# A prologue that gives every group of input rows its own landing place, splits x in chunks on two engines, and multiplies the first slot's low columns before the last parameter rows

## What is computed

```python
def rglru_mixer(x, conv_buf, h0, in_w, conv_w, conv_b, r_w, r_b, i_w, i_b, lam, out_w):
    gate, u = jnp.split(x @ in_w, 2, axis=-1)
    u, new_buf = causal_dwconv(u, conv_buf, conv_w, conv_b)
    ub = u.reshape(bsz, t, LRU_BLOCKS, LRU_BS)
    r = jax.nn.sigmoid(jnp.einsum('btnk,nkj->btnj', ub, r_w).reshape(bsz, t, LRU_W) + r_b)
    ig = jax.nn.sigmoid(jnp.einsum('btnk,nkj->btnj', ub, i_w).reshape(bsz, t, LRU_W) + i_b)
    log_a = -LRU_C * r.astype(f32) * jax.nn.softplus(-lam.astype(f32))
    ...
    y = (h.astype(x.dtype) * jax.nn.silu(gate)) @ out_w
```

## Time and profile before

| | us |
|---|---|
| median of 3 runs | 1575.88 (1572.28 to 1580.37) |
| the profiled execution | 1573.39 |
| its span, first to last instruction | 1571.7 |
| TensorE busy (matmuls) | 1434.7 (91%) |
| VectorE busy | 974.7 (62%) |
| ScalarE busy | 723.0 (46%) |
| GpSimd busy | 608.3 (39%) |
| mean granted TensorE clock | 0.940 |

### The profile page before, as it was taken

The page is one execution under the profiler, slowest core; times in us unless marked ns, Lnnn a source line. Parts: engine busy times, 40 slices in busy tenths (PEclk is TensorE's granted clock), DMA queues, the critical chain, the costliest instruction groups (busy, mean ns, idle before and its releaser), DMA issues.

```text
span 1571.7 us, 33403 instructions
## 1 busy us (share of the span) xinstructions
PE 1434.7 (91%) x12546; PEld 1306.7 (83%) x12546; DVE 974.7 (62%) x2099; ACT 723.0 (46%) x1403; POOL 608.3 (39%) x728
## 2 busy tenths in 40 slices
PE   5999889999999998888799999999999799799985
PEld 4998779888888875778789989888988599799885
DVE  4467572446555665545658778867977743646755
ACT  1577333335444444422535455454544532467721
POOL 1466343222222220146325435434445545256531
PEclk6999979999999998999799999999999799899987
DMA  3322233567667666632122414324333242222221
GB/s 119 85 74 72 65 89 109 176 196 222 214 205 226 207 193 218 196 95 76 45 73 65 114 45 125 108 69 114 108 84 95 62 116 84 81 73 79 79 58 58
DMA packets 282537, 179.72 MB, mean 114 GB/s; under 512 B 18906, under 2 KB 280826, under 8 KB 282376
## 3 DMA queue, kind: packets, MB, share of 16 engines
q1 hardware_dynamic: 282376, 177.58, 38.3%
HBM read 160.67 MB, written 16.86 MB: 113 GB/s over the span
## 4 chain that ended last, share of the span: by engine, by line
PE 57%; DVE 21%; ACT 7%; issue 6%; SPq 3%; POOL 3%; DMA 2%; DVEq 0%; ACTq 0%; POOLq 0%
PE proj L197 7%; PE proj L1755 7%; PE proj_lo L1755 7%; PE proj_lo L197 6%; PE proj L986 5%; PE proj_lo L986 4%; DVE conv L2257 3%; PE r L997 3%; PE x L1081 2%; POOL w_low L172 2%; PE s L1042 2%; DVE m L2286 1%; SPq L890 1%; PE s L1009 1%; DVE m L2302 1%
## 5 line engine op out<-in xcount | busy, mean ns | idle before, releaser
L172 POOL TENSOR_TENSOR w_low<-w_raw,w_high 128x256 fp32r<-128x256 f32 x608 | 526.2, 896 | 854.4 <-ACT w_high L163 854.4
L163 ACT ACTIVATE w_high<-w_raw 128x1024 fp32r<-128x1024 f32 x152 | 160.5, 1056 | 142.8 <-PE proj_lo L1755 51.2
L1755 PE MATMUL proj<-xh,w_high 128*128 128x288 f32 x440 | 136.3, 310 | 4.4 <-POOL w_low L172 3.0
L1755 PE MATMUL proj<-xh,w_low 128*128 128x288 f32 x440 | 131.1, 298 | 0.0
L1755 PE MATMUL proj<-xl,w_high 128*128 128x288 f32 x440 | 130.9, 298 | 0.0
L1755 PE MATMUL proj_lo<-xh,w_high 128*128 128x256 f32 x440 | 128.9, 293 | 0.0
L1755 PE MATMUL proj_lo<-xl,w_high 128*128 128x256 f32 x440 | 125.7, 286 | 0.0
L1755 PE MATMUL proj_lo<-xh,w_low 128*128 128x256 f32 x440 | 124.7, 283 | 0.0
L1755 PEld LDWEIGHTS proj_lo<-xh,w_high 128*128 128x128 f32 x440 | 84.8, 193 | 10.0 <-issue 10.0
L1755 PEld LDWEIGHTS proj<-xh,w_high 128*128 128x128 f32 x440 | 84.7, 192 | 8.5 <-POOL w_low L172 5.0
L1755 PEld LDWEIGHTS proj_lo<-xl,w_high 128*128 128x128 f32 x440 | 84.8, 193 | 0.0
(11 more groups left out here) (477 smaller groups left out, 4338.4 us busy)
## 6 DMA issues: line engine op xcount, KB each, us to landing
k_pages<-in_cache_k SPq DMA_DIRECT2D x256, 128.0 KB, 2.6
v_pages<-in_cache_v SPq DMA_DIRECT2D x256, 128.0 KB, 2.4
w_raw<-in_c_in_w SPq DMA_DIRECT2D x48, 512.0 KB, 3.9
w_raw<-in_a_in_w SPq DMA_DIRECT2D x32, 512.0 KB, 3.9
w_raw<-in_b_in_w SPq DMA_DIRECT2D x32, 512.0 KB, 4.2
w_raw<-in_a_out_w SPq DMA_DIRECT2D x16, 512.0 KB, 3.9
st<-in_state_ssd_h SPq DMA_DIRECT2D x16, 512.0 KB, 4.7
out_ssd_h_sample<-st SPq DMA_DIRECT2D x16, 512.0 KB, 6.4
```

Of the source, the lines that this page charges most:

```text
L163: act.activation(k.wh[par][:], k.raw[par][:], ACT.Copy).then_inc(k.sem["w_hi"], 1)
L172: step = pool.tensor_tensor(k.wl[par][:, tiles, :], k.raw[par][:, tiles, :], k.wh[par][:, tiles, :], ALU.subtract)
L1755: mm = pe.matmul(out, w[par][:, i, :], x[:, i, cols], start=first and opens and i == 0 and n == 0, stop=last and i == KT - 1 and n == 2, s ...
```

## The change

The twelve jobs become seven: five of x, one of both "a" groups (80 rows), one of the "c" and "m" groups (126 rows). Each lands in its own place, `k.land`, in memory that nothing else uses yet (the tile `branch`), so that SyncE waits for no transpose, and each has its own semaphore. The order of the loads is x0, x1, first weight block, x2, x3, sample rows, 14 loads of "a" rows, second weight block, 15 loads of "c" and "m" rows.

Copies of x out of PSUM are shared: VectorE takes chunks 0, 2 and 4, ScalarE 1 and 3. ScalarE rounds each chunk by itself and VectorE subtracts each by itself. TensorE transposes the five jobs of x and the "a" job, multiplies the first slot's low columns as soon as two chunks are split, transposes the "mc" job, and multiplies the high columns when all five are. ScalarE rounds the second weight block before the exponential and copies the "mc" job out of PSUM; VectorE copies the "a" job. GpSimd subtracts the second weight block ahead of its first copy of history columns (`history(0)`). The first gates' matmuls wait for ScalarE's copies out of `s`.

```diff
@@ -110,6 +110,7 @@
     k.gh, k.gl = k.g[:, 0:KT, :], k.g[:, KT:2 * KT, :]
     k.sq = [sb(f"sq{j}", [P, 2, T]) for j in range(2)]
     k.rows = [q.rearrange("p a t -> p (a t)")[:, 0:D] for q in k.sq]
+    k.land = [k.out.rearrange("p a t -> p (a t)")[:, n * D:(n + 1) * D] for n in range(7)]
     k.raw = [sb(f"w_raw{j}", [P, KT, P]) for j in range(2)]
     k.wh = [sb(f"w_high{j}", [P, KT, P], F32R) for j in range(2)]
     k.wl = [sb(f"w_low{j}", [P, KT, P], F32R) for j in range(2)]
@@ -226,36 +227,56 @@
-def row_jobs(a):
...
+X_JOB = range(CH)
+A_JOB, MC_JOB = CH, CH + 1
+A_ROWS, C_ROWS, M_ROWS = 40, 29, 10
+JOB_ROWS = [P] * QB + [NS, 2 * A_ROWS, 4 * C_ROWS + M_ROWS]
+JOB_LANDED = [f"x{c}_landed" for c in X_JOB] + ["a_landed", "mc_landed"]
+def x_rows(a, c):
+    if c == QB:
+        return [(0, NS, a["x_sample"].rearrange("b t d -> (b t) d"))]
+    return [(0, P, a["x_prompt"].rearrange("b t d -> (b t) d")[c * P:(c + 1) * P, :])]
+def a_rows(a):
+    parts = []
     for j in range(2):
+        at = A_ROWS * j
         one = [a["a_conv_b"], a["a_gate_r_b"], a["a_gate_i_b"], a["a_lambda"]]
-        jobs.append(("a", j, 40, [(0, 4, a["a_conv_w"][j])]
...
+        parts += [(at, 4, a["a_conv_w"][j])] + [(at + 4 + n, 1, v[j:j + 1, :]) for n, v in enumerate(one)]
+        parts += [(at + 8, 24, a["state_lru_conv"][j].rearrange("b k d -> (b k) d")), (at + 32, 8, a["state_lru_h"][j])]
+    return parts
+def mc_rows(a):
+    at = 4 * C_ROWS
+    parts = [(at, 4, a["ln_g"]), (at + 4, 4, a["ln_b"]), (at + 8, 2, a["c_norm_w"].rearrange("a (r d) -> (a r) d", r=2))]
     for q in range(CONV_C // D):
-        cols = slice(q * D, (q + 1) * D)
-        jobs.append(("c", q, 29, [(0, 4, a["c_conv_w"][0][:, cols]), (4, 1, a["c_conv_b"][:, cols]),
-                                  (5, 24, a["state_ssd_conv"][0].rearrange("b k d -> (b k) d")[:, cols])]))
-    return jobs
+        at, cols = C_ROWS * q, slice(q * D, (q + 1) * D)
+        parts += [(at, 4, a["c_conv_w"][0][:, cols]), (at + 4, 1, a["c_conv_b"][:, cols]),
+                  (at + 5, 24, a["state_ssd_conv"][0].rearrange("b k d -> (b k) d")[:, cols])]
+    return parts
 def prologue_sync(sp, k, a):
-    landed = [0, 0]
...
+    def rows(job, parts):
         for at, n, src in parts:
-            sp.dma_start(k.rows[j % 2][at:at + n, :], src).then_inc(k.sem[f"rows_landed{j % 2}"], 16)
+            sp.dma_start(k.land[job][at:at + n, :], src).then_inc(k.sem[JOB_LANDED[job]], 16)
+    rows(0, x_rows(a, 0))
+    rows(1, x_rows(a, 1))
+    load_slot(sp, k, 0, 0, a_slot(a, 0, 0))
+    for c in range(2, CH):
+        rows(c, x_rows(a, c))
+    rows(A_JOB, a_rows(a))
+    load_slot(sp, k, 1, 1, a_slot(a, 0, 1))
+    rows(MC_JOB, mc_rows(a))
 def a_slot(a, j, n):
@@ -276,38 +297,83 @@
     split_low(pool, k, 0, 0)
-def prologue_tensor(pe, k, a):
+def prologue_tensor(pe, k):
     sem = k.sem
+    def turn(job, parts):
+        n, bank = JOB_ROWS[job], (k.s, k.r)[job % 2]
+        pe.wait_ge(sem[JOB_LANDED[job]], 16 * parts)
+        for i in range(KT):
+            t = pe.transpose(bank[:, i // 4, (i % 4) * n:(i % 4) * n + n], k.land[job][0:n, i * P:(i + 1) * P], k.ident[0:n, 0:n])
+        t.then_inc(sem["rows_turned"], 1)
+    def first_slot(out, cols):
+        for i in range(KT):
+            for n, (w, m) in enumerate(((k.wh, k.xh), (k.wh, k.xl), (k.wl, k.xh))):
+                mm = pe.matmul(out, w[0][:, i, :], m[:, i, cols], start=i == 0 and n == 0, stop=i == KT - 1 and n == 2)
+        return mm
     pe.wait_ge(sem["consts"], 1)
-    landed = [0, 0]
...
+    turn(0, 1)
+    turn(1, 1)
+    pe.wait_ge(sem["rows_read"], 1)
+    turn(2, 1)
+    pe.wait_ge(sem["rows_copied"], 1)
+    turn(3, 1)
+    pe.wait_ge(sem["rows_read"], 2)
+    turn(4, 1)
+    pe.wait_ge(sem["rows_copied"], 2)
+    turn(A_JOB, 14)
+    pe.wait_ge(sem["w_lo"], 2)
+    pe.wait_ge(sem["x_part"], 2)
+    first_slot(k.proj_lo[:, 0:HALF], slice(0, HALF))
+    pe.wait_ge(sem["rows_read"], 3)
+    turn(MC_JOB, 15)
+    pe.wait_ge(sem["x_part"], CH)
+    first_slot(k.proj[:, 0, 0:T - HALF], slice(HALF, T)).then_inc(sem["pe_slot"], 1)
+def chunk(c):
+    return slice(c * P, min(c * P + P, T))
+def turned(k, job, at, n):
+    bank, rows = (k.s, k.r)[job % 2], JOB_ROWS[job]
+    return bank[:, :, 0:4 * rows].rearrange("p b (i n) -> p b i n", i=4)[:, :, :, at:at + n]
+def by_banks(dst):
+    return dst.rearrange("p (b i) n -> p b i n", b=2)
+def prologue_vector(dve, k, chain):
     sem = k.sem
+    def copied(c):
+        dve.wait_ge(sem["rows_turned"], c + 1)
+        dve.tensor_copy(by_banks(k.xT[:, :, chunk(c)]), turned(k, c, 0, JOB_ROWS[c])).then_inc(sem["rows_read"], 1)
+    def low(c):
+        dve.wait_ge(sem["x_split"], c + 1)
+        dve.tensor_tensor(k.xl[:, :, chunk(c)], k.xT[:, :, chunk(c)], k.xh[:, :, chunk(c)], ALU.subtract).then_inc(sem["x_part"], 1)
     dve.wait_ge(sem["consts"], 1)
-    for j, (kind, c, n, _) in enumerate(row_jobs(a)):
...
+    copied(0)
+    low(0)
+    copied(2)
+    low(1)
+    copied(4)
+    low(2)
+    low(3)
+    low(4)
+    dve.sem_inc(sem["x_ready"], 1)
+    dve.wait_ge(sem["rows_turned"], A_JOB + 1)
+    for j in range(2):
+        dve.tensor_copy(by_banks(k.par_a[j][:]), turned(k, A_JOB, A_ROWS * j, A_ROWS)).then_inc(sem["rows_read"], 1)
+    dve.wait_ge(sem["rows_read"], 5)
     for j in range(2):
         d = k.par_d[j]
         chain(dve.tensor_scalar(d[:, 0:2, :].rearrange("p c i -> p i c"), k.par_a[j][:, :, 5:7], 0.5, None, ALU.mult))
@@ -342,13 +408,31 @@
     act.activation(tmp[:, 0], tmp[:, 0], ACT.Exp, scale=-1.0).then_inc(k.sem["sp_out"], 1)
-def prologue_scalar(act, k, a):
+def prologue_scalar(act, k):
+    sem = k.sem
+    def copied(c):
+        act.wait_ge(sem["rows_turned"], c + 1)
+        act.activation(by_banks(k.xT[:, :, chunk(c)]), turned(k, c, 0, P), ACT.Copy).then_inc(sem["rows_copied"], 1)
+    def high(c, copies, count):
+        act.wait_ge(sem[copies], count)
+        act.activation(k.xh[:, :, chunk(c)], k.xT[:, :, chunk(c)], ACT.Copy).then_inc(sem["x_split"], 1)
     split_high(act, k, 0, 0, 0)
-    act.wait_ge(k.sem["rows_read"], CH)
-    act.activation(k.xh[:], k.xT[:], ACT.Copy).then_inc(k.sem["x_split"], 1)
+    copied(1)
+    high(0, "rows_read", 1)
+    high(1, "rows_copied", 1)
+    copied(3)
+    high(2, "rows_read", 2)
+    high(3, "rows_copied", 2)
+    high(4, "rows_read", 3)
+    split_high(act, k, 1, 0, 1)
     softplus_scalar(act, k, k.spa[:, :, 0:2 * KT], 1)
+    act.wait_ge(sem["rows_turned"], MC_JOB + 1)
+    for q in range(CONV_C // D):
+        act.activation(by_banks(k.par_c[:, q * KT:(q + 1) * KT, :]), turned(k, MC_JOB, C_ROWS * q, C_ROWS), ACT.Copy)
+    act.activation(by_banks(k.par_m[:]), turned(k, MC_JOB, 4 * C_ROWS, M_ROWS), ACT.Copy).then_inc(sem["rows_copied"], 1)
 def a_sync(sp, k, a, o, j, nxt):
@@ -400,17 +484,18 @@
         pe.wait_ge(sem["gw_landed"], 64 * n + 64)
         pe.wait_ge(sem["conv_done"], n + 1)
         pe.wait_ge(sem["ti_ready"], n)
+        if n == 0:
+            pe.wait_ge(sem["rows_copied"], 3)
         for g in range(2):
             pe.matmul(k.s[:, g, :], k.gw[:, g, :], k.cx[:, 0:SEQ], start=True, stop=True)
         for g in range(2):
             mm = pe.matmul(k.r[:, 0, g * NS:g * NS + NS], k.gw[:, g, :], k.cx[:, SEQ:T], start=True, stop=True)
         mm.then_inc(sem["gates_done"], 1)
-    if j == 0:
-        pe.wait_ge(sem["x_ready"], 1)
     for i in range(KT):
-        if i == 0 and j:
-            multiply_new_x(pe, k, s0, u0, 3)
+        if i == 0:
+            if j:
+                multiply_new_x(pe, k, s0, u0, 3)
         else:
             multiply_slot(pe, k, s0 + 2 * i, 0, u0 + 2 * i, u0 // 2 + i, 0, k.xh, k.xl,
                           (lambda mm: gates(i - 1)) if i else None)
@@ -520,8 +605,7 @@
         act.activation(k.gh[:, i, :], k.hg[i % 2][:], ACT.Copy).then_inc(sem["a_high"], 1)
     if j == 0:
-        act.wait_ge(sem["rows_read"], CH + 2)
-        split(1)
+        act.wait_ge(sem["rows_read"], 5)
     for i in range(KT + 1):
         if i:
             rates(i - 1)
@@ -647,9 +731,9 @@
         pool.tensor_copy(k.tails[:, i, 0:HN].rearrange("p (b t) -> p b t", t=HIST), rows).then_inc(sem["a_tails"], 1)
     if j == 0:
-        pool.wait_ge(sem["rows_read"], CH + 2)
+        low(1)
+        pool.wait_ge(sem["rows_read"], 5)
         history(0)
-        low(1)
     else:
         low(1)
         pool.wait_ge(sem["x_ready"], 4)
```

More of the change, by code:

```diff
@@ L131, in allocate @@
     names = """w_landed0 w_landed1 w_hi w_lo pe_slot p_evac0 p_evac1 s_evac x_ready x_tile
-        rows_landed0 rows_landed1 rows_turned rows_read consts chain_act chain_dve chain_pool
-        sp_in sp_out params x_split
+        x0_landed x1_landed x2_landed x3_landed x4_landed a_landed mc_landed rows_turned rows_read rows_copied consts chain_act chain_dve chain_pool
+        sp_in sp_out params x_split x_part
```

(36 more changed lines are left out.)

14 lines of the change are left out of this document (removed).

## The result

| | before | after |
|---|---|---|
| median, us (lowest to highest) | 1577.06 (1572.28 to 1580.37), 4 runs | 1560.84 (1558.99 to 1562.84), 4 runs |
| span of the profiled execution | 1571.7 | 1561.1 |
| end of the first slot | 42.10 | 25.70 |

The ratio is 0.9896 [0.9881, 0.9912]: the changed kernel is faster by 1.0%, 16.2 us between the medians. The forecast was 1556 in a range of 1551 to 1564.

A forecast was written before the change was run, and what follows sets the result against it. The prediction took one slack-free chain of waits up to the first slot's end as the bound; ending it at 23.8 instead of 42.10 saves 18.3 us, giving 1555.1, or 1557.6 by the median; forecast 1556, range 1551 to 1564.

The forecast's parts named there:

- The bound and the mechanism: Prologue: the first forty microseconds are one chain without slack; the rearranged loads, splits and TensorE order shorten it.
- The carry to the end: After the first slot: what its end gains, 18.3 us, is carried to the end of the program.
- the gain is taken back later: Rival, later stages: one paced by transfers alone starts no earlier; about 1574; chance 0.07, shared with a missed TensorE wait.
- The median-based estimate: Whole program: 1555.1 from the profiled execution, raised by the 2.5 the median lies above it, gives 1557.6.
- The end of the slot: First projection slot: its last matmul ends at 23.8 us (22.6 to 25.8) against 42.10, 18.3 us earlier.
- Loads: SyncE's queue: about 1.5 us per 512 KB; x2 lands at 9.2, x3 10.8, first parameter group 12.2, second 15.
- Rows in a crowd: Rival, prologue: 29 unpaced small loads land late, the slot ends at 29.3, 12.8 us gained, 1561; chance 0.10.
- The clock: TensorE, low columns: 2.84 us at full clock or 5.1 at half; 4.0 taken since the level was open.
- The weights late: Rival, first slots: GpSimd's weight splits slow beside VectorE, TensorE idles at half clock; six slots give 1584; chance 0.04.

The follow-up runs named there:

- e2_x_whole: Changed kernel with x rounded and subtracted whole again and all five copies on VectorE; median of 6 runs 1566.86 us, ratio to before 0.9945.
- the repeat: The changed kernel measured once more with no edit; median of 6 runs 1557.15 us, ratio to before 0.9876.
- e1_mc_first: Changed kernel with the 126-row job transposed ahead of the first slot's low columns instead of behind them; one run, 1562.0 us.
- e6_fill: Changed kernel with TensorE's waits ahead of x0, x2 and x3 filled with transposes of the identity; one run, 1559.51 us.
- e5_fewer_loads: Changed kernel with the same parameter rows in 13 loads instead of 29; median of 4 runs 1555.41 us, ratio to before 0.9868.
- e4_rows_late: Changed kernel with small loads held until x3 has landed and the 80-row job behind the low columns; one run, 1561.45 us.
- e3_paced: Changed kernel with SyncE again waiting for the transposes of the job two before, landing places kept; one run, 1562.52 us.

## Why the prediction was right, and what was mis-sized

**The bound and the mechanism** were right. The first forty microseconds were one chain, and each of the three parts (loads that don't wait, x in chunks on two engines, low columns ahead of the second parameter group) carries its share, shown at the end of the slot by undoing each.

**The carry to the end** was right: the stretch from the first slot's end to the attention layer is 197.2 before and after, and in `e2_x_whole`, which gives 5.2 us back, it is 197.5. That rival ("the gain is taken back later") fell. In the span the gain is blurred (10.6 us in the first profile, 20.0 in the repeat), because the later layers vary by several microseconds between executions. The median-based estimate, 1557.6, lies between the medians of the two sets of runs, 1560.84 and 1557.15, half a microsecond from the second. That closeness is luck: the first slot gave 16.4 us, not the 18.3 of the estimate, and the two sets lie 16.2 and 19.9 us below the kernel before, a spread wider than the miss.

**The end of the slot** was put at 23.8 (22.6 to 25.8) and came at 25.70: 1.9 of the 18.3 us were not there. The term that was mis-sized is "Loads":

| step | predicted | measured |
|---|---|---|
| x3 landed | 10.8 | 12.59; 10.5 to 11.7 in the repeat, `e1_mc_first`, `e2_x_whole` and `e6_fill` |
| "a" rows landed | 12.2 | 14.96 (repeat), 15.33 (`e6_fill`) |
| low columns start | 15.5 | 17.11; 16.39 in the repeat |
| second weight block rounded | 17.5 | 18.9; 18.5 in the repeat, 19.2 in `e1_mc_first` |
| "mc" rows landed | 15 | 21.39 (`e1_mc_first`) |
| low columns take | 4.0 | 4.53; 5.20 in the repeat |
| 126-row job takes | 1.1 | 0.86 |

The low columns' start is 1.6 late, their length 0.5 over, the 126-row job 0.2 under. In the first profile it is x3, 1.8 late, that holds the start; in the other runs x3 is near its place, and the "a" rows, 2.8 late in the repeat, hold it instead. I had carried 1.5 us for each 512 KB on through the small loads, as if only bytes counted. The windows of the changed kernel show otherwise (length; busy PE, PEld, DVE, ACT, POOL; granted clock, DMA share, GB/s):

```profile
8.00:9.00 1.00, 0.35 (x2) 0.00 (x0) 0.00 (x0) 0.90 (x1) 0.00 (x0) 1.00 1.01 410
...
10.00:11.00 1.00, 1.00 (x6) 1.00 (x6) 0.00 (x0) 1.00 (x3) 1.00 (x2) 1.00 1.09 174
11.00:12.00 1.00, 0.71 (x4) 0.31 (x2) 0.96 (x1) 0.96 (x2) 1.00 (x2) 1.00 1.04 141
```

The DMA engines are as busy throughout, but from 10 to 12 us they move 174 and 141 GB/s, against 410 from 8 to 9.

**Rows in a crowd** thus had the right mechanism and I gave it 0.10. It did not give its 29.3 because it put the 126-row job at 25, and those rows landed at 21.4, while the low columns still ran. The order of TensorE's work, not the speed of the loads, saved the forecast. The total does not favour the forecast: this rival's time was 1561, and the first set's median, 1560.84, is nearer to it than to 1556. The two times are 5 us apart and the change's own two medians 3.7, so it is the end of the slot (25.70, against 23.8 and 29.3) that tells the forecast from this rival, and not the total.

**The clock** was left open with a mean of both levels, and that was the right way to treat it. x2 took 1.94 us in one execution of the changed kernel and 1.07 in another; the slot ended at 25.70 and 25.73, because what the faster turns saved went into the wait for the "a" rows and into low columns at half clock throughout (5.20 against 4.53). In both, a wait of TensorE for a load stood ahead of low columns at half clock. The granted clock in the windows above is 1.00, while x2's transposes, from 9.77 on, took 1.94, and it still reads 1.00 from 17 to 20 us, where the low-column matmuls start every 0.21 us. The Trainium skill, "TensorE: Matmul & The Clock Gate", section "What's actually happening", calls the throttled level the default; the durations agree with it, and the column's first stretch does not.

**The weights late** did not happen. GpSimd's splits took 3.77 and 3.00 us beside VectorE's subtractions against 2.77 beside none, and the second was done 3.75 us before the slot ended. The Trainium skill, "GPSIMD Engine Reference", section "1. Specifications", states that GpSimd shares its SBUF interfaces with VectorE's instructions of two SBUF inputs. The trace agrees (2.77 against 3.77, and 6.35 in `e2_x_whole`), but the splits here had room.

**The 2 us at the first landmark.** The stretch to the attention layer was 2 us shorter in the repeat (195.4) and in `e1_mc_first` (195.0) than in the other profiles of the change (197.2 to 197.5). TensorE's clock goes with it. The 24 low-column matmuls of layer 0's output projection took 5.10 us in the first profile, at a granted 0.56, and 3.11 in the repeat and in `e1_mc_first`, at 1.00; the other profiles of the change have 4.6 to 5.2. A sum over x for the layer's LayerNorm then took 1.08 us in the first profile and 0.55 and 0.56 in those two. The kernel before has 3.10 for the projection but 1.08 for that sum, and 0.95 where the others have 0.54. So 197.2 before and 197.2 after are equal to some 2 us, and to a tenth by chance.

**Open.** It was not settled what makes the small rows move slowly. With 13 loads the rate from 10 to 13 us was about as low (152 to 168 GB/s in `e5_fewer_loads`), so the number of loads is not it. The packets of the slow stretch are smaller (300 in 0.32 MB from 10 to 12 us in the changed kernel, against 112 in 0.41 MB from 8 to 9), but that alone is not it either: in `e4_rows_late` 638 packets in 0.32 MB moved at 325 GB/s from 17 to 18 us.

## What to carry to other kernels

A prologue in which one engine's chain starts everything is worth writing as a list of landings, and each engine's in-order program should hold back only what the next matmul reads: here a job that nothing needed yet, moved behind 24 matmuls, hid a load that came 6 us later than planned. Price a burst of small loads from its issue time and the backlog ahead of it, not from its bytes alone (2.81 us from last issue to landing behind a drained queue, 7.76 behind a full one), and join rows that lie next to each other into one load. To see whether a gain survives, compare a landmark behind the change before comparing totals: the first landmark showed 16.4 and 18.2 us in two profiles, where the span showed 10.6 and 20.0, and `e2_x_whole`, whose slot ended 5.2 us later, had a shorter profiled span (1559.0) than the first profile of the change (1561.1).

## What was not expected of the hardware

- 29 small loads queued without pacing behind the loads of x and weights landed up to 7.76 us after their last issue (`e1_mc_first`), against 2.81 in `e4_rows_late`, equally unpaced but with x landed, 2.08 in `e3_paced` and 2.36 before. In the changed kernel the rate fell to 141 GB/s at a DMA share of 1.04.
- ScalarE copies 128x1024 out of PSUM in 1.01 to 1.02 us, VectorE in 1.21 to 1.23.
- GpSimd's split of four pieces takes 2.77 us beside no subtraction, 3.77 beside chunked subtractions, and 6.35 beside the whole 4.69 us one, ending 2.66 us behind it. That subtraction took VectorE the same 4.69 as without GpSimd beside it, but its 16-wide instructions beside the split went from 0.17 or 0.18 to 0.66.
